# Two transformer blocks on one core: the second half of the first modulation by quarters, weight parts ahead of the convolutions, 32-column sums

## The reference

```python
c_act = jax.nn.silu(c)
mod = (c_act @ w_ada[l] + b_ada[l])[:, None, :]
shift1, scale1, gate1, shift2, scale2, gate2 = jnp.split(mod, 6, axis=-1)
h = rms_norm(x, norm1_w[l]) * (1.0 + scale1) + shift1
proj = h @ w_in[l]
gq, gk, gv, gz, ga, gb, sq, sk, sv = jnp.split(proj, split_points, axis=-1)
qkv = jax.nn.silu(causal_depthwise_conv(jnp.concatenate([gq, gk, gv], axis=-1), conv_w[l]))
...
g = -jnp.exp(a_log[l].astype(jnp.float32)) * jax.nn.softplus(ga.astype(jnp.float32) + dt_bias[l].astype(jnp.float32))
```

## Time and profile before

| what | value |
|---|---|
| median of 3 runs | 991.53 us (991.39 to 992.0) |
| the profiled execution | 990.9 us, of which the span of its instructions is 989.1 us |
| PE busy | 978.5 us (99%) |
| DVE busy | 607.8 us (61%) |
| ACT busy | 476.8 us (48%) |
| granted clock of PE, mean | 0.996 |

### The profile page before, as it was taken

One profiled execution on the slowest core, in us unless ns is written; L12 is line 12 of the kernel. 1 busy time (PEld: TensorE's weight loads), 2 busy tenths in 40 slices (PEclk: granted clock), 3 DMA queues, 4 the chain that ended last, 5 costly groups with the idle time before them and its releaser, 6 DMA issues.

```text
span 989.1 us, 15628 instructions
## 1 busy us (share of the span) xinstructions
PE 978.5 (99%) x6703; PEld 847.0 (86%) x6703; DVE 607.8 (61%) x750; ACT 476.8 (48%) x640; POOL 36.8 (4%) x37
## 2 busy tenths in 40 slices
PE   9999999999999999999999999999999999999998
PEld 6799988978888888999888888889999888888886
DVE  2589988775665454787754545365876663545444
ACT  3485277454343435533354344446655563435343
POOL 0000560010000000000000000000000000000000
PEclk9999999999999999999999999999999999999999
DMA  9757324775767354446544645454643435454621
GB/s 345 284 191 259 122 87 151 270 243 214 278 217 285 132 211 172 171 171 214 211 145 153 216 167 206 177 191 153 226 156 130 139 144 185 180 204 166 216 86 43
DMA packets 31588, 185.70 MB, mean 188 GB/s; under 512 B 3040, under 2 KB 5536, under 8 KB 10784
## 3 DMA queue, kind: packets, MB, share of 16 engines
q1 hardware_dynamic: 29984, 180.37, 51.0%
q0 software_dynamic: 832, 3.17, 1.0%
q10 hardware_dynamic: 704, 1.17, 0.3%
HBM read 183.62 MB, written 1.07 MB: 187 GB/s over the span
## 4 chain that ended last, share of the span: by engine, by line
PE 98%; DVE 1%; ACT 0%; issue 0%; POOL 0%; DVEq 0%; POOLq 0%
PE bank L1706 51%; PE acc L1706 43%; PE bank L2308 1%; PE bank L2086 1%; PE bank L1802 0%; PE acc L1802 0%; PE acc L2086 0%; PE bank L2166 0%; PE bank L1979 0%; DVE inv_b L1391 0%; DVE norm_tmp L1511 0%; DVE silu_and_hid L1510 0%; DVE inv_b L1384 0%; PE acc L2316 0%; DVE X_inv L1435 0%
## 5 line engine op out<-in xcount | busy, mean ns | idle before, releaser
L1075 DVE TENSOR_TENSOR w_lo<-raw,w_hi 128x2048 fp32r<-128x2048 f32 x144 | 326.9, 2289 | 146.2 <-ACT w_hi L675 146.1
L1706 PE MATMUL bank<-w_hi,h_parts 128*128 128x512 f32 x1056 | 333.5, 391 | 1.3 <-DVE h_parts L1152 1.3
L675 ACT ACTIVATE w_hi<-raw 128x2048 fp32r<-128x2048 f32 x144 | 271.5, 1909 | 102.3 <-PE acc L1706 70.9
L1706 PEld LDWEIGHTS bank<-w_hi,h_parts 128*128 128x128 f32 x1056 | 198.2, 188 | 44.6 <-issue 2.0
L1706 PE MATMUL bank<-w_lo,h_parts 128*128 128x512 f32 x528 | 205.5, 389 | 0.0
L1706 PE MATMUL acc<-h_parts,w_hi 128*128 128x256 f32 x928 | 170.8, 286 | 0.6 <-DVE h_parts L1127 0.6
L1706 PEld LDWEIGHTS acc<-h_parts,w_hi 128*128 128x128 f32 x928 | 143.5, 190 | 5.3 <-issue 3.3
L1706 PE MATMUL acc<-h_parts,w_lo 128*128 128x256 f32 x464 | 131.2, 283 | 0.0
L1706 PE MATMUL acc<-w_hi,o_hi 128*128 128x512 f32 x296 | 119.1, 402 | 0.0
L1706 PEld LDWEIGHTS bank<-w_lo,h_parts 128*128 128x128 f32 x528 | 99.2, 188 | 19.8
L1706 PE MATMUL acc<-w_hi,o_lo 128*128 128x512 f32 x296 | 115.6, 391 | 0.0
(11 more groups left out here) (370 smaller groups left out, 993.3 us busy)
## 6 DMA issues: line engine op xcount, KB each, us to landing
raw<-stream SPq DMA_DIRECT2D x162, 1024.0 KB, 5.1
AT<-stream SPq DMA_DIRECT2D x2, 1024.0 KB, 11.8
qkT<-stream SPq DMA_DIRECT2D x2, 1024.0 KB, 13.0
X_inv<-stream SPq DMA_DIRECT2D x2, 1024.0 KB, 14.2
keys_queries<-stream SPq DMA_DIRECT2D x4, 512.0 KB, 12.4
t_tables<-t_scratch POOLq DMA_DIRECT2D x1, 2048.0 KB, 10.2
x_res<-x_in SPq DMA_DIRECT2D x2, 512.0 KB, 5.2
t_tables<-t_scratch POOLq DMA_DIRECT2D x1, 1024.0 KB, 12.4
```

Source lines behind the costliest of these rows:

```text
L675: act.activation(high_of(w), raw_of(r), ACT.Copy).then_inc(s.hi_ready, 1)
L1075: dve.tensor_tensor(low_of(w), raw_of(weight_load(w)), high_of(w), ALU.subtract).then_inc(s.lo_ready, 1)
L1706: return pe.matmul(o, l, r, start=start, stop=stop, skip_group_check=True)
```

## The change

- The second half of the modulation is fetched and computed in two quarters (features 512 to 767, 768 to 1023), scale and shift of a quarter as one 1 MB part each, in pieces of 256 columns. All four go through `ada_quarter`, ACT and `row_sums`; `last_columns` remains for the first half only, and seven `warm` matmuls of the second half are gone.
- Block 2 is loaded between the quarters. Blocks 2 and 3 are split in quarters too (`FIRST_WEIGHTS = 4`). PE multiplies blocks 0, 1 and 2 with tiles 0 to 3, then 4 and 5, then 6 and 7; the gate columns are made in the same three steps, in another bank (`B[3]`).
- In the loop over blocks 0 to 5, ACT and DVE make the parts of block w + 3 (before: w + 2) ahead of the copy and the convolution of block w.
- The right side of the sums of squares of the first norm, of `row_sums` and of `last_columns` is 32 columns wide.

Constants and the transfers:

```diff
+WIDE = 32
-FIRST_WEIGHTS = 2
+FIRST_WEIGHTS = 4
+EARLY_LOADS = 3
+FEATURES = ((0, 4), (4, 6), (6, 8))
...
+            def load_quarter(q, u):
+                i = 2 * (q - 2) + u
+                if i < 3:
+                    sp.wait_ge(s.ada_used, i + 1)
+                else:
+                    sp.wait_ge(s.rows_summed, 2)
+                c = 256 * q + (0 if u else D)
+                sp.dma_start(ada_raw[i].rearrange("p (k c) -> p k c", k=KD),
+                             stream[0:KD, :, c:c + 256].rearrange("k p c -> p k c")).then_inc(ada_landed[i], 16)
...
             load(1)
-            for i in range(4):
-                load_ada(1, i)
-            sp.wait_ge(ada_landed[2], 32)
-            for i in range(2, len(LOADS)):
+            load_quarter(2, 0)
+            load_quarter(2, 1)
+            load(2)
+            load_quarter(3, 0)
+            load_quarter(3, 1)
+            for i in range(EARLY_LOADS, len(LOADS)):
                 load(i)
```

In the list of ACT:

```diff
             mod_rows_copy(1, 0)
+            first_highs(2, (0, 1))
             mod_rows_copy(1, 1)
-            h_high(0, range(4, KD))
+            h_high(0, range(4, 6))
+            first_highs(2, (2, 3))
+            mod_rows_copy(2, 0)
+            mod_rows_copy(2, 1)
+            h_high(0, range(6, KD))
...
             for w in range(6):
-                hi(w + 2)
+                if w + 3 < FIRST_WEIGHTS:
+                    first_highs(w + 3, (0, 1, 2, 3))
+                else:
+                    hi(w + 3)
```

In the list of DVE:

```diff
             first_scales(1)
+            first_lows(2, (0, 1))
             first_shifts(1)
-            for k in range(4, KD):
-                first_scaled(k)
-                if k > 4:
-                    first_low(k - 1)
-            first_low(KD - 1)
+            first_scaled(4)
+            first_scaled(5)
+            first_low(4)
+            first_low(5)
+            first_lows(2, (2, 3))
+            first_scales(2)
+            first_shifts(2)
+            first_scaled(6)
+            first_scaled(7)
+            first_low(6)
+            first_low(7)
...
-                lo(w + 2)
+                if w + 3 < FIRST_WEIGHTS:
+                    first_lows(w + 3, (0, 1, 2, 3))
+                else:
+                    lo(w + 3)
```

In the list of PE:

```diff
+            def column_part(w, ks):
+                bank = A[w]
                 wh = high_of(w)
                 wl = low_of(w)
                 for k in ks:
+                    if k < 6:
                         pe.wait_ge(s.first_lo, 3 * w + k // 2 + 1)
+                    else:
+                        pe.wait_ge(s.lo_ready, w + 1)
                     pe.wait_ge(s.h_lo_ready, k + 1)
...
+            def ada_quarter(q, u):
+                i = 2 * (q - 2) + u
+                pe.wait_ge(ada_landed[i], 32)
+                pe.wait_ge(s.rows_copied, i + 1)
+                for k in range(KD):
+                    at = 32 * (k % 4)
+                    ins = mm(B[u][at:at + 32, 0:256], c_columns[:, k, :], ada_raw[i][:, 256 * k:256 * k + 256], k < 4, k >= 4)
+                ins.then_inc(s.ada_used, 1)
...
-                        ins = by_halves(STAT[:, at:at + 1], ada_raw[3][:, 512 * k + P * j:512 * k + P * j + P],
-                                        c_act[:, 4 + k:5 + k], False, k == 3)
+                        ins = by_halves(STAT[:, at:at + WIDE], ada_raw[3][:, 512 * k + P * j:512 * k + P * j + P],
+                                        c_columns[:, 4 + k, :], False, k == 3)
...
-            column_half(0, A[0], range(4))
-            ada(1, 0)
-            column_half(1, A[1], range(2))
-            ada(1, 1)
-            column_half(1, A[1], range(2, 4))
+            column_part(0, range(0, 4))
+            ada_quarter(2, 0)
+            column_part(1, range(0, 2))
             row_sums(1, 0)
-            ada(1, 2)
-            warm(3)
+            column_part(1, range(2, 4))
+            ada_quarter(2, 1)
+            gab_part(range(0, 4))
             row_sums(1, 1)
-            last_columns(1)
-            warm(4)
+            column_part(2, range(0, 4))
+            ada_quarter(3, 0)
+            column_part(0, range(4, 6))
+            row_sums(2, 0)
+            ada_quarter(3, 1)
+            column_part(1, range(4, 6))
+            row_sums(2, 1)
+            column_part(2, range(4, 6))
+            gab_part(range(4, 6))
...
-                if w < 2:
-                    column_half(w, A[w], range(4, KD))
+                if w < EARLY_LOADS:
+                    column_part(w, range(6, KD))
+                elif w < FIRST_WEIGHTS:
+                    column_part(w, range(KD))
```

More of the change, by code:

```diff
@@ L403, in build @@
         flat = lambda b: b.rearrange("p a b -> p (a b)")
-        mod_rows = [[inv_b[:, 1024 * i + 512 * u:1024 * i + 512 * u + 512] for u in range(2)] for i in range(2)]
+        mod_rows = [[inv_b[:, P * (2 * a + (b - a) * u):P * (2 * a + (b - a) * (u + 1))] for u in range(2)] for a, b in FEATURES]
         ada_raw = [flat(AT), flat(qkT), flat(X), flat(kqb[:, 0:8, :])]
@@ L711, in _, with mod_rows_copy @@
             root(0)
-            def mod_rows_copy(half, u):
-                act.wait_ge(s.ada_used, 3 * half + (3 if u else 2))
-                act.activation(mod_rows[half][u], B[u][:, :], ACT.Copy).then_inc(s.rows_copied, 1)
+            def mod_rows_copy(part, u):
+                a, b = FEATURES[part]
+                act.wait_ge(s.ada_used, 2 * part + u + 2)
+                act.activation(mod_rows[part][u], B[u][:, 0:P * (b - a)], ACT.Copy).then_inc(s.rows_copied, 1)
             def first_highs(w, quarters):
@@ L720, in first_highs @@
                 act.wait_ge(raw_landed[r % RING], (r // RING + 1) * 16)
+                if FORMER[w] is not None:
+                    act.wait_ge(s.block_used, STEP[FORMER[w]])
                 for q in quarters:
@@ L1808, in square_sums @@
                 pe.wait_ge(s.squared, 8 * n + m + 1)
+                width = 1 if n else WIDE
                 for t in range(TT):
-                    ins = by_halves(B[3][:, t:t + 1], nt[:, m, P * t:P * t + P], ones, m == 0 and t == 0, m == KD - 1)
+                    ins = by_halves(B[3][:, width * t:width * t + width], nt[:, m, P * t:P * t + P], ones.broadcast_to([P, width]),
+                                    m == 0 and t == 0, m == KD - 1)
                 return ins
@@ L1825, in _, with ada_half @@
             two = lambda b: b[:, :].rearrange("p (a b) -> p a b", a=2)
[L1827 to L1831, removed]
+            def ada_half(i):
+                pe.wait_ge(ada_landed[i], 16)
                 for k in range(4):
@@ new lines, in row_sums @@
+            def row_sums(part, u):
+                a, b = FEATURES[part]
+                pe.wait_ge(s.rows_copied, 2 * part + u + 1)
+                if part + u:
+                    pe.wait_ge(s.mod_ready, 2 * part + u)
+                for j in range(b - a):
+                    at = WIDE * (2 * a + (b - a) * u + j)
+                    ins = by_halves(STAT[:, at:at + WIDE], mod_rows[part][u][:, P * j:P * j + P], ones.broadcast_to([P, WIDE]),
+                                    j == 0, part + 1 - u > 0)
+                if part + 1 - u:
@@ L1857, in last_columns, with gab_part @@
                 ins.then_inc(s.rows_summed, 1)
+            def gab_part(ks):
+                pe.wait_ge(s.x_scaled, KD)
+                pe.wait_ge(s.gab_lo, 1)
+                for k in ks:
+                    pe.wait_ge(s.h_lo_ready, k + 1)
+                    a, b = gab_wh[:, 16 * k:16 * k + 16], gab_wl[:, 16 * k:16 * k + 16]
+                    ins = three(B[3][0:16, 0:T], a, b, h_hi[:, k, :], h_lo[:, k, :], k == 0, k == KD - 1)
+                if ks[-1] == KD - 1:
+                    ins.then_inc(s.gab_product, 1)
@@ L1926, in _ @@
                 if w == 0:
-                    pe.wait_ge(s.gab_lo, 1)
-                    for k in range(KD):
-                        a, b = gab_wh[:, 16 * k:16 * k + 16], gab_wl[:, 16 * k:16 * k + 16]
-                        ins = three(B[0][0:16, 0:T], a, b, h_hi[:, k, :], h_lo[:, k, :], k == 0, k == KD - 1)
-                    ins.then_inc(s.gab_product, 1)
+                    gab_part(range(6, KD))
                     pe.wait_ge(s.t5_loaded, 48)
```

59 lines of the change are left out of this document (26 added, 33 removed).

## The result

The changed kernel takes 993.83 us (median of 22 runs, 993.11 to 996.6), the kernel before 992.13 in the runs beside it (22 runs, 989.35 to 995.07): a ratio of 1.0024, interval [1.0015, 1.0033]. It is slower by 0.24%, about 2.4 us. The profiled executions say the same: 993.25 against 990.9 us. The two fastest runs lie 3.8 us apart; why that is more than the ratio says stands at the end.

The account below looks back on a forecast made before the run. PE bounds the kernel (busy 978.5 of 989.1 us), with DVE's chain 1.4 us behind it. 990.9 + 1.0 (head sums) + 1.5 (clock) = 993.4 profiled; the median, 0.6 above, 994.0; range 989.6 to 995.8.

Parts of the forecast that it names:

- DVE's chain: From block 0 to the decay: DVE's work sets when PE begins block 6's head sums; slack before was 1.4 us.
- PE's lead: PE would end block 2 at about 52.3 instead of 56.8, a lead of 4.5 us, all lost in two waits.
- Wide products, clock at 21 us: At `last_columns`: 32-column products cost 0.032 us each, the clock stays up, first column matmul at 24.49 instead of 24.83.
- Transfers: Early weight loads: 3.0 us per 1 MB part in 1 KB pieces; quarters at 27.6, 30.6, 36.3, 39.3, block 2 at 33.3.
- Block 0 ready: 47.6: PE's early work: block 0 ready at 47.6 instead of 44.2, 3.4 us later, with next row sums 0.4 late.
- First convolution: On DVE: starts at 50.75 instead of 46.45, 4.3 us later, behind block 3's high part and four low parts.
- The chain from there: 27.6: DVE from first convolution to end of `decay`: 25.7 us of work plus 1.9 us idle, 27.6 in all.
- Head sums: +1.0: Middle of block 6: PE begins the head sums at 78.4 to 78.5 instead of 77.45, 1.0 us later.
- Waits of PE: 2.4 and 2.9: PE stands 2.4 us for the gates near 64 and 2.9 us for `decay` near 75.
- The clock: +1.5: Behind the wait for `decay`: the clock falls and meets dense work, costing 1.5 us, ends 0 and +3.
- the rule of the Trainium skill: At PE's waits: bursts with waits between them go cold each time; used to forecast a fall behind the second wait.
- The range of 6.2 us: Forecast time from 989.6 to 995.8 us, leaving out a tenth below and less above.

Follow-up runs that it names:

- e7: Kernel before plus two additions of zeros (128 x 512) on DVE at the start of w = 3; 990.98 us, ratio 0.9999.
- e10: Kernel before plus two additions (128 x 512) on DVE at w = 4, where DVE has no idle time; 994.29 us, ratio 1.0027.
- e9: Changed kernel plus two additions (128 x 512) on DVE at w = 4, where DVE has no idle time; 996.22 us, ratio 1.0045.
- e1: Changed kernel with the loop's weight parts in the old order (block w + 2), quarters and wide sums kept; 992.62 us, ratio 1.0007.
- e2: Changed kernel with 10 multiplications of zeros (about 2.2 us) on PE ahead of its wait for the gates; 996.25 us, ratio 1.0041.
- e8: Changed kernel with PE's waits for the gates and for the decay each one step later in its list; 994.62 us, ratio 1.0025.
- after: The changed kernel itself, against the kernel before; 993.83 us, ratio 1.0024.
- e4: Changed kernel with one-column right sides again in place of 32 columns; 995.31 us, ratio 1.0047.
- e3: Kernel before with nothing but the 32-column right sides; 990.13 us, ratio 0.9986.
- e5: Changed kernel with weight parts in the old order and PE finishing block 0 ahead of block 2's later tiles; 990.0 us, ratio 0.9988.
- e12: e5 with ACT's high part of w = 5 moved ahead of its wait for the gates' logarithm; 989.29 us, ratio 0.9973.
- e6: Changed kernel plus two additions of zeros (128 x 512) on DVE at the start of w = 3; 995.23 us, ratio 1.0038.

## Why the prediction was right, and where its steps were not

The time (993.83 against 994.0) and the sign are right, and the cause is the one given: DVE's chain, started later, sets PE's head sums, and PE's lead turns into two waits. The first convolution starts 4.96 us later than before; 4.04 of them are block 0's, the rest are the low parts of block 3 ahead of it (3.14 us from block 0 to the convolution, 2.22 before, when `lo(2)` stood there). But the sum is right by luck: two terms were off, in opposite directions. The delay of the head sums was 1.15 us more than forecast, the clock cost 1.5 less, and the profiled execution came out at 993.25 where 993.4 was forecast.

- *Wide products, clock at 21 us.* Right. 2.01 us for 64 products of 32 columns, 0.031 each (taken 0.032); first column matmul at 24.40 (24.49). But the link from one-column products to the fall is looser than the prediction took it: e7 and e10 have the products without the fall.
- *Transfers.* Right. The second part into AT landed at 12.3 + 15.4 = 27.7 (27.6); block 2 at 33.3 (33.3), the last quarter at 39.2 (39.3).
- *Block 0 ready: 47.6, was 48.27.* The row sums that were to wait until 34.8 did not: their copy ended at 34.74, and PE, late by its own work, came only at 35.09. It went on at 35.5 (35.2), 0.3 late. From there the 78 matmuls took 3.04 + 1.63 + 1.61 + 1.62 + 0.69 + 1.43 = 10.0 us where I took 78 x 0.12 = 9.4, and the two parts and two row sums 2.7 where I took 3.0. The first groups in the chain:

```profile
35.52 3.04 PE acc L1738 x24
38.56 1.00 PE bank L1738 x16
39.56 1.63 PE acc L1738 x12
41.19 1.36 PE bank L1738 x24
42.54 1.61 PE acc L1738 x12
```

  0.12 is the mean of a run of 144; here a group of 12 behind a part or row sums took 0.134 to 0.136 each, and the last one, behind gate matmuls of the same width, 0.119 (1.43 / 12). The change from one kind to the next cost about 0.2 us a group.
- *First convolution.* 3.1 us behind block 0, as computed. It came at 51.41 instead of 50.75 because block 0 was late, and for no other reason.
- *The chain from there: 27.6, was 28.14.* Work as counted; the second convolution waited 0.85 (0.4), then 1.30 and 0.21 as said. ACT had the SiLU that it waited for behind the copy of block 1, and that behind the end of the first convolution (54.80), with a table load of 1.28 in between.
- *Head sums: +1.0, was +2.15.* The two misses above, 0.7 and 0.5. e9 confirms the mechanism with a dose (and e10, with e7 beside it, shows that the same dose does not reach these head sums in the kernel before), e1 with the parts put back, e2 and e8 by PE's side having no effect on `kds`.
- *Waits of PE: 2.4 and 2.9, were 2.74 and 1.06.* The second is short because of the next point.
- *The clock: +1.5, was 0 in the profiled execution.* This is the step that failed. I looked for a fall behind the second wait and none behind the first, of 2.4 us. It fell behind the first, for 3.4 us, and made 67.51 to 78.55 take 11.0 us where 9.3 were computed: this came out of the second wait. The price itself was right: in e2, where the fall to 1.2 GHz came behind the second wait, it was 12.51 - 10.99 = 1.5 (the product written in the prediction, 3.3 x (1 - 0.12 / 0.21), is 1.4). In other executions of the changed kernel the clock did cost time: eight of the 22 were at a granted clock of 0.994 and took 994.7 to 996.6; where it fell in them no trace shows.

Of what hung on the rule of the Trainium skill (TensorE: Matmul & The Clock Gate, section "HAM oscillation — how this bites in real kernels"): by it the clock falls at such waits, and most of the traces agree: it fell behind waits of 2.7 us at 69 (after), 2.6 us at 80 (e2) and 81 (e8), and within one of 4.1 (e9). But e9's wait of 2.9 us for the gates had no fall behind it, and e1 and e4 have one behind waits of 1.3 and 1.0 us. What I added to it, which of two waits would be hit, was a guess, and no run shows what decides it.

The range of 6.2 us was justified less by the terms than by the clock. The kernel before ran from 989.3 to 995.3 at granted clocks from 0.999 down to 0.990, and profiles of it or with one addition show falls at 11.7, 21, 37 or 39 us. With wide products alone (e3) the runs lie between 989.6 and 991.6, at 0.997 to 1.0; the fastest are no faster than those of the kernel before. So the width gains where a fall would have come, and nothing in the executions that have none. That is the likely reason why the fastest runs of the two kernels lie 3.8 us apart and the ratio says 2.4: the wide products spare the changed kernel falls which the kernel before has in many of its executions, and not in its fastest. Between e3 and after, two profiles without a fall ahead of 66 us, the head sums move from 75.87 to 79.61, by 3.7 us, and their ratios lie 3.8 us apart. So the quarters and the new order cost some 3.8 us. The prediction started from a profile with a fall at 21 us in it, and therefore saw less.

## What to carry to other kernels

When two engines run in lockstep, find the chain of the slower one and count what is put ahead of its start; a lead for the bounding engine is worth nothing beyond the slack of that chain, and here it was spent in two waits, behind one of which the clock fell. When the work is reordered, finish first the block that the other engine starts from (e5), and look for idle time in the helper chain that a third engine causes (e12). For small groups of matmuls take the mean of small groups, not of the longest run. And before a clock is taken from one profile, compare several executions: here falls came at other places from one to the next.

## What was not expected of the hardware

- The fall of the clock moves with the place of a wait, and whether it costs anything depends on what comes behind: 0 us in front of another wait (after), 1.5 and 2.5 us where it began behind or within the last one (e2, e9).
- At 2.4 GHz 64 products of 32 columns took 2.06 us (e3) and 64 of one column 2.03 (e10). The ten profiles with 32 columns have no fall in the first 66 us, the four with one column each have one or two in the first 45, but not always at these products.
- e1, e4, e6 and e12 show a fall at 146 to 155 us, where the others show none, within 0.6 us of the end of a wait of 1.2 us which all of them have (it ends at 151.58 in after, at 150.47 in e1). What decides it was not tried.
